# An fp32 transformer kernel on one core: VectorE's product takes the scale of the norm, ScalarE writes only the high part, and the residual is made later

## The reference

```python
for l in range(DEPTH):                      # DEPTH = 2, alpha = 4 ** 0.25
    y = _mla(...) if l == 0 else _swa(...)  # attention, ends with a product o @ w_o
    x = _layernorm(alpha * x + y, ln_mix_g[l], ln_mix_b[l])
    x = _layernorm(alpha * x + _mlp(x, w_up, w_down), ln_mlp_g[l], ln_mlp_b[l])
# _layernorm: (x - mean) * rsqrt(var + eps) * g + b, over the 1024 features
# _mlp: relu(x @ w_up) ** 2 @ w_down
```

## Time and profile before

| | |
|---|---|
| median of three runs | 1906.15 us (1903.37 to 1907.59) |
| the profiled execution, its own time | 1903.75 us |
| its span | 1901.7 us |
| instructions | 22411 |
| VectorE (DVE) busy | 992.5 us, 52% |
| ScalarE (ACT) busy | 663.2 us, 35% |
| GpSimd (POOL) busy | 32.0 us, 2% |
| mean granted clock of TensorE | 0.963 of full speed |

### The profile page before, as it was taken

One profiled execution on the slowest core, in us unless ns is written; L12 is line 12 of the kernel. 1 busy time (PEld: TensorE's weight loads), 2 busy tenths in 40 slices (PEclk: granted clock), 3 DMA queues, 4 the chain that ended last, 5 costly groups with the idle time before them and its releaser, 6 DMA issues.

```text
span 1901.7 us, 22411 instructions
## 1 busy us (share of the span) xinstructions
PE 1818.5 (96%) x9112; PEld 1535.9 (81%) x9112; DVE 992.5 (52%) x1421; ACT 663.2 (35%) x919; POOL 32.0 (2%) x42
## 2 busy tenths in 40 slices
PE   7999989999998999989999999898999999999998
PEld 6787978888888887878888888787878788888886
DVE  3666643434346556653334247655566666256554
ACT  3454341322233446342223133323452322132332
POOL 0000000000000113000000000000000000000000
PEclk9899999999999897999999999897989999999999
DMA  7211223223221110312222322120102222422331
GB/s 270 89 67 45 89 89 111 89 89 110 89 89 67 67 67 1 111 67 102 94 92 88 111 89 89 58 92 28 70 20 84 105 88 93 151 89 91 116 147 67
DMA packets 28287, 169.66 MB, mean 89 GB/s; under 512 B 2800, under 2 KB 7088, under 8 KB 9136
## 3 DMA queue, kind: packets, MB, share of 16 engines
q1 hardware_dynamic: 22448, 156.44, 23.2%
q10 hardware_dynamic: 5760, 12.08, 1.9%
HBM read 166.39 MB, written 5.27 MB: 90 GB/s over the span
## 4 chain that ended last, share of the span: by engine, by line
PE 86%; DVE 7%; ACT 5%; issue 1%; DMA 0%; POOL 0%; DVEq 0%; ACTq 0%
PE ps L1477 28%; PE ps L1479 27%; PE ps L1478 27%; PE ps L1598 2%; DVE w_lo L814 2%; ACT y L562 1%; ACT w_hi L408 1%; ACT s_prob L432 1%; ACT act_hi L570 1%; PE ps L1550 0%; DVE s_pt_lo L814 0%; DVE s_prob L856 0%; PE ps L1872 0%; PE ps L1541 0%; DVE y L965 0%
## 5 line engine op out<-in xcount | busy, mean ns | idle before, releaser
L1477 PE MATMUL ps<-act_hi,w_lo 128*128 128x512 f32 (+1 forms) x1424 | 533.5, 375 | 40.6 <-DVE w_lo L814 22.0
L1478 PE MATMUL ps<-act_hi,w_hi 128*128 128x512 f32 (+1 forms) x1424 | 527.9, 371 | 0.0
L1479 PE MATMUL ps<-act_lo,w_hi 128*128 128x512 f32 (+1 forms) x1424 | 527.8, 371 | 0.0
L408 ACT ACTIVATE w_hi<-stage 128x2048 fp32r<-128x2048 f32 (+4 forms) x147 | 267.3, 1819 | 386.1 <-PE ps L1479 385.4
L814 DVE TENSOR_TENSOR w_lo<-stage,w_hi 128x2048 fp32r<-128x2048 f32 (+5 forms) x151 | 322.5, 2137 | 88.6 <-ACT w_hi L408 88.1
L1477 PEld LDWEIGHTS ps<-act_hi,w_lo 128*128 128x128 f32 x1424 | 272.7, 191 | 89.8 <-issue 28.6
L1479 PEld LDWEIGHTS ps<-act_lo,w_hi 128*128 128x128 f32 x1424 | 272.3, 191 | 45.4
L1478 PEld LDWEIGHTS ps<-act_hi,w_hi 128*128 128x128 f32 x1424 | 272.7, 192 | 44.1
L1477 PE MATMUL ps<-hid_hi,w_lo 128*128 128x512 f32 (+1 forms) x576 | 213.0, 370 | 2.1 <-DVE w_lo L814 2.1
L1479 PE MATMUL ps<-hid_lo,w_hi 128*128 128x512 f32 (+1 forms) x576 | 211.4, 367 | 0.0
L1478 PE MATMUL ps<-hid_hi,w_hi 128*128 128x512 f32 (+1 forms) x576 | 209.7, 364 | 0.0
(11 more groups left out here) (279 smaller groups left out, 2315.5 us busy)
## 6 DMA issues: line engine op xcount, KB each, us to landing
stage<-slabs SPq DMA_DIRECT2D x147, 1024.0 KB, 4.8
bias_rows<-bias_line ACTq DMA_DIRECT2D x1, 3072.0 KB, 19.0
y<-x_t ACTq DMA_DIRECT2D x4, 512.0 KB, 8.4
strips<-bias_rows ACTq DMA_DIRECT2D x2, 1024.0 KB, 6.2
strips<-dilated ACTq DMA_DIRECT2D x2, 1024.0 KB, 5.0
out<-y ACTq DMA_DIRECT2D x4, 512.0 KB, 2.6
stage<-slabs SPq DMA_DIRECT2D x4, 256.0 KB, 7.7
cossin<-rope SPq DMA_DIRECT2D x1, 512.0 KB, 11.6
```

The lines of the kernel that those rows point to most:

```text
L408: nc.scalar.activation(w_hi[p][:, 0:w], stage[s][:, 0:w], ACT.Copy).then_inc(cast_hi, 1)
L1477: mm(out, l_lo, r_hi, start=start, stop=False, skip_group_check=shared)
L1478: mm(out, l_hi, r_hi, start=False, stop=False, skip_group_check=shared)
L1479: return mm(out, l_hi, r_lo, start=False, stop=stop, skip_group_check=shared)
```

## The change

In norms 0, 1 and 2 (all with `last=False`):
- `scale`: for each pair of tiles VectorE runs two `scalar_tensor_tensor` on 128x256, y = y * gain * inverse root, gain being a column of `vec` and the root in PSUM, in place of one 128x512 product.
- `apply`: ScalarE writes `act_hi` = y + offset directly, two 128x256 instructions, in place of two on y, a wait and a 128x512 copy. y no longer gets the offset.
- `lo`: VectorE runs two `scalar_tensor_tensor` on 128x256, `act_lo` = (y + offset) - `act_hi`, in place of one 128x512 subtraction.
- `residual`: behind half 1's `apply`, ScalarE computes a small tile `abeta` = ALPHA * offset (128x8), waits for it, and then runs eight 128x512 instructions y = ALPHA * y + `abeta`. Each waits until VectorE has made the low parts of its pair; the last signals `x_scaled`.
- The out products that were added with the factor ALPHA in the MLPs and before norm 2 are added without it; VectorE waits for `x_scaled` before the first of them. Those before norm 0 keep the factor, as the input x is not scaled.

Norm 3 keeps its instructions.

```diff
+        abeta = keep("abeta", [P, 8])
...
@@ scalar: layer_norm
                     for p in range(4):
                         act.wait_ge(norm_z, 8 * n + 4 * h + p + 1)
+                        if not last:
+                            for t in (2 * p, 2 * p + 1):
+                                ins = nc.scalar.activation(act_hi[:, t, c], y[:, t, c], ACT.Identity,
+                                                           bias=col(beta, t))
+                            ins.then_inc(norm_hi, 1)
+                            continue
                         for t in (2 * p, 2 * p + 1):
                             ins = nc.scalar.activation(y[:, t, c], y[:, t, c], ACT.Identity, bias=col(beta, t),
                                                        scale=col(gain, t))
                         link(ins)
-                        if last:
-                            for t in (2 * p, 2 * p + 1):
-                                ins = nc.scalar.activation(act_hi[:, t, c], y[:, t, c], ACT.Copy,
-                                                           scale=col("g_mix", t))
-                        else:
-                            ins = nc.scalar.activation(act_hi[:, 2 * p:2 * p + 2, c], y[:, 2 * p:2 * p + 2, c],
-                                                       ACT.Copy)
+                        for t in (2 * p, 2 * p + 1):
+                            ins = nc.scalar.activation(act_hi[:, t, c], y[:, t, c], ACT.Copy, scale=col("g_mix", t))
                         ins.then_inc(norm_hi, 1)
+
+                def residual(gen):
+
+                    link(nc.scalar.activation(abeta[:, :], vec[:, VEC[beta]:VEC[beta] + 8], ACT.Copy, scale=ALPHA))
+                    for t in range(KT):
+                        act.wait_ge(act_ready, gen + 8 + 2 * (t // 2) + 2)
+                        ins = nc.scalar.activation(y[:, t, :], y[:, t, :], ACT.Identity, bias=abeta[:, t:t + 1],
+                                                   scale=ALPHA)
+                    ins.then_inc(x_scaled, 1)
...
                 apply(1)
+                if not last:
+                    residual((LN_0, LN_1, LN_2)[n])
@@ vector: layer_norm
                 def scale(h, p):
                     c, bank = half_cols(h), 5 + 2 * h
+                    if not last:
+                        for t in (2 * p, 2 * p + 1):
+                            ins = nc.vector.scalar_tensor_tensor(y[:, t, c], y[:, t, c], col(gain, t),
+                                                                 ps[:, bank, 0:HALF], ALU.mult, ALU.mult)
+                        ins.then_inc(norm_z, 1)
+                        return
...
-                        pair_ = slice(2 * p, 2 * p + 2)
-                        split(act_lo[:, pair_, c], y[:, pair_, c], act_hi[:, pair_, c]).then_inc(act_ready, 2)
+                        for t in (2 * p, 2 * p + 1):
+                            split_scaled(act_lo[:, t, c], y[:, t, c], col(beta, t), act_hi[:, t, c], ALU.add)\
+                                .then_inc(act_ready, 1)
@@ vector: mlp
+                dve.wait_ge(x_scaled, 2 * layer + 1)
                 for j in range(4):
-                    add_out(first + 4 + j, 2 * j, scaled=True)
+                    add_out(first + 4 + j, 2 * j)
@@ vector: the calls
-            layer_norm(SWA_OUT, 2, scaled=True)
+            dve.wait_ge(x_scaled, 2)
+            layer_norm(SWA_OUT, 2, "mix_g1", "mix_b1")
```

More of the change, by code:

```diff
@@ L250, in program @@
         x_landed = [sem(f"x_landed{i}") for i in range(4)]
-        x_hi = sem("x_hi")
+        x_hi, x_scaled = sem("x_hi"), sem("x_scaled")
         const_landed, p_landed = sem("const_landed"), sem("p_landed")
@@ L917, in add_out, with layer_norm @@
                 add(t, slice(0, T), ps[:, b:b + 2, :], scaled).then_inc(slab_read, 1)
-            def layer_norm(first, n, scaled=False, last=False):
+            def layer_norm(first, n, gain, beta, scaled=False, last=False):
                 for j in range(2):
@@ L1156, in _ @@
                 mla_out(u0 + 3)
-            layer_norm(MLA_OUT, 0, scaled=True)
+            layer_norm(MLA_OUT, 0, "mix_g0", "mix_b0", scaled=True)
             mlp(MLP0, 0)
-            layer_norm(MLP0 + 28, 1)
+            layer_norm(MLP0 + 28, 1, "mlp_g0", "mlp_b0")
             g = SWA_KV
@@ L1206, in _ @@
                 swa_out(u0 // 2 + 3)
-            layer_norm(SWA_OUT, 2, scaled=True)
+            dve.wait_ge(x_scaled, 2)
+            layer_norm(SWA_OUT, 2, "mix_g1", "mix_b1")
             mlp(MLP1, 1)
-            layer_norm(MLP1 + 28, 3, last=True)
+            layer_norm(MLP1 + 28, 3, "mlp_g1", "mlp_b1", last=True)
             cast(CONV + 2)
```

## The result

Eleven runs of the changed kernel have a median of 1913.96 us, eleven of the kernel before on the same chip 1903.64 us. The ratio is 1.0045, 95% interval 1.0029 to 1.0061: **slower by 8.6 us** (5.5 to 11.6). The forecast was 1904.8 and a small gain. The profiled execution took 1913.96 us, span 1911.9, against 1903.75 and 1901.7 before.

The account below looks back on a forecast made before the run. TensorE, busy 96% of the span, was taken as the bound, so only its waits around the norms could change: -0.06, -0.85 and -0.36 make -1.3 us, 1904.8 against the median 1906.15. Range 1901.0 to 1910.0.

Parts of the forecast that it names:

- Half 0: First half of norms 0 to 2: the slab's low part starts 7.3 us after the first scale, 0.85 us earlier.
- Norm 1's wait: TensorE's wait for VectorE's add of the last out product: 2.1 instead of 2.98 us, 0.85 gained in full.
- Half 1: Second half of norms 0 to 2: first low part 2.77 us after the scale, TensorE restarting 0.50 us earlier.
- The wait of 0.52: TensorE's wait at 230.10 in norm 0 for a weight slab's low part: 0.52 us gained, likewise in norm 2.
- Slab 49: Behind norm 1: its low part ready 0.46 us later against half 1's scale, TensorE losing and gaining nothing.
- One-column prices: ScalarE instructions with one column operand: 0.91 us a pair for the new high part, 0.63 a residual step.
- The relu: First slab's relu on ScalarE, behind the residual: 0.46 us later in norm 0, 0.16 in norm 2, delaying TensorE's restart.
- the sum of -1.3 us: All terms over the three norms: -0.06 in norm 0, -0.85 in norm 1, -0.36 in norm 2.
- the out products there lose their constant factor: Out products in the MLPs and before norm 2: no TensorE wait ends on one, so costed at nothing.
- ScalarE as the new bound: Rival: residual at two-column price, first relu waits 1.56 us, TensorE's waits 3.8 and 3.5; +5.6, 1911.8 us, chance 0.11.
- The clock falls in the lengthened waits: Rival: waits of 2.9 (norm 0) and 2.6 us (norm 2) lower TensorE's clock; 1906.6 or 1908.3 us, chance 0.25.
- The clock is kept where it fell: Rival: shorter waits, norm 1's 3.52 to 3.0 and norm 2's 4.41 to 3.9, save clock loss; -4.7, 1901.4 us, chance 0.13.

Follow-up runs that it names:

- after_in_place: The changed kernel with abeta in a 64-byte tile replacing table_mark and mark, so later tiles lie as before the change; 1903.35 us, ratio 0.9991 to the kernel before.
- base128: The kernel before with tiles rden and negsink moved to the free end of memory, so hid_hi begins 128 bytes behind a multiple of 2048; 1900.62 us, ratio 0.9986.
- pad32: The kernel before with one unused tile of 128x8 (32 bytes a partition) where the change puts abeta; 1912.06 us, ratio 1.0049.
- late_early: late_residual with the first slab behind each of norms 0 to 2 cast right behind half 1's last parts, ahead of the relu; 1895.74 us, ratio 0.9948 to the kernel before.
- late_residual: after_in_place with ScalarE's eight residual steps moved behind the second up slab's cast (norms 0, 2) or slab 50's (norm 1); 1900.27 us, ratio 0.9978 to the kernel before.
- front32: The kernel before with an unused 32-byte tile ahead of every other tile, moving staging, weight and act tiles too; 1904.41 us, ratio 1.0003.
- act32: The kernel before with act_hi, act_lo, y and the small tiles moved by 32 bytes, weights and hid_hi left in place; 1929.43 us, ratio 1.0129.

## Why the prediction was wrong

**The steps that held.** Half 0: 7.19 us for 7.3. Norm 1's wait: 2.07 us for 2.1, in part by luck. Its release came 0.96 us sooner behind the first scale (601.21 - 589.24 = 11.97, before 12.93) where 0.85 was forecast. In after_in_place that is 11.96, but the wait is 2.38, as TensorE came to it sooner: slab 47 lies in the third pair of weight tiles (see base128), and its triples take 340 ns there and some 355 in the changed kernel, which moved that pair as well. Half 1: the first matmul 2.87 us behind the scale (239.19 to 242.06) for 2.92. The wait of 0.52 gone. Slab 49: TensorE began its product 16.36 us behind the scale of half 1 (626.96 - 610.60), before 16.42 (623.15 - 606.73), so nothing lost and nothing gained, as forecast. One-column prices: 0.91 a pair, residual steps 0.62 apart for 0.63. By the figures of the Trainium skill ("ScalarE: Activation LUTs", under "What ACT_TABLE_LOAD costs") the step is 0.61, an estimate and nearer still; the trace agrees with its rule that each pointer operand adds some 93 ns (a pair 0.91 with one, 1.09 with two). The relu: 0.23 us later in norm 0 for 0.46, since the last high part ended 0.10 sooner than worked out (6.03 behind the scale for 6.13) and the steps took 0.11 less together. With `abeta` in place the sum of -1.3 us met -1.7, interval -3.8 to +0.2.

**The step that failed** is one that the prediction did not price: "the out products there lose their constant factor, with the same elements", "No DMA is added", and nothing on the tile that the change adds. `abeta` is described as a small tile of 128x8, the prediction prices the instruction that writes it, and nowhere is it asked what it moves: the pace of TensorE's products on other tiles was a term put at nothing without a reason. "These waits are all the change can touch" is the sentence that was false: TensorE's pace in products 100 us away could be touched too, through addresses. pad32 shows that this alone costs 9.3 us (6.9 to 11.6), as much as the change lost.

**The rivals.** None of them had this mechanism. The one that ended slower, ScalarE as the new bound, came nearest in time, 1911.8, for a reason that the trace refutes: steps at 0.62 us, the wait at 257.91 at 2.12 us and not 3.8. "The clock falls in the lengthened waits": the wait in norm 0 grew to 2.12 us and not to 2.9, the one in norm 2 not at all, and the clock stayed up behind both. In norm 0 the reason is the clock itself: from 242 to 250 its mean was 0.79 before and is 0.71 now, which makes TensorE some 0.6 us later at the wait. The stretches (us, busy and instructions of PE, PEld, DVE, ACT, POOL, granted clock, DMA share, GB/s) answer to the earlier trace rows:

```profile
242.00:246.00 4.00, 3.94 (x18) 3.97 (x19) 3.81 (x10) 2.57 (x7) 0.00 (x0) 0.50 0.00 0
258.00:262.00 4.00, 4.00 (x18) 3.31 (x19) 2.29 (x3) 2.87 (x2) 0.00 (x0) 1.00 0.71 250
601.00:605.00 4.00, 3.79 (x19) 3.80 (x20) 1.76 (x5) 0.63 (x1) 0.00 (x0) 0.58 0.51 211
613.00:618.00 5.00, 4.53 (x36) 4.44 (x37) 4.36 (x11) 3.37 (x8) 0.00 (x0) 1.00 0.00 0
```

In after_in_place, where norm 2's wait did grow to 2.91 us, the clock did fall behind it, as this rival has it:

```profile
839.00:845.00 6.00, 5.59 (x18) 4.45 (x19) 4.30 (x4) 2.86 (x2) 0.00 (x0) 0.72 0.51 175
```

In the changed kernel the clock fell behind a wait of 2.07 us (601) and stayed behind one of 2.99 (613), where before it had stayed behind 2.98 and fallen behind 3.52. The prediction's reasoning from the longest harmless wait does not hold: the length of one wait does not decide. What does for a single wait, these runs leave open. The Trainium skill's advice against long idle gaps ("TensorE: Matmul & The Clock Gate", under "Why this matters for your kernels") is borne out in part: the falls in these rows came with waits, but the wait of 2.99 us brought none. "The clock is kept where it fell", priced at 1.7 us in norm 1, came true there (613) and gained nothing: TensorE got through the slabs sooner and then waited 1.56 us for slab 49, whose low part comes behind the residual. Over the whole kernel it evened out: mean clock 0.963 before, 0.962 after.

**The range** was wrong for the same cause: it was built from the bounds of terms that held, and had no term for what stood outside them. The 0.12 for slower stood on another cause alone. (The 0.72 for "same" is 0.45, 0.25 and 0.06 less the 0.03 and 0.01 given to the two sides, not 0.01 a side.)

## What to carry to other kernels

A new tile is an edit to every tile allocated after it. Before a change that adds one is judged by its instructions, compare the addresses of the matmul operands, and time the kernel with the tile alone; better, put small tiles into a gap or at the end. When a change costs more than its own stages show, compare the starts of the same event, product by product, over the whole span: a loss that grows by an equal step at products the change does not touch is a change of pace, not a wait.

When engines stand idle behind a stage, look for work whose inputs and place are long free. Here one cast behind each norm, moved ahead of the relu, was worth 5.7 us by the ratios of late_early and late_residual, more than the 1.7 of the arithmetic.

## What the runs showed that was not expected

- TensorE's pace at 128x512 depends on where the streamed operand lies against tiles allocated before it, taken within 2048 bytes: 681 ns for the three matmuls at a distance of 0 from the weights (act; hid in base128: 680), 687 at 320, 700 at 352 and 384, 703 at 416, and some 700 for act at 32. At 128x256 the order differs: 360 ns at 0, 353 at 320 (hid). That 2048 is the period fits all these but was not varied.
- Both operands' places count. front32 moved weights and act together, and nothing changed; act32 moved act and left the weights; and base128 moved the third pair of weight tiles and left act, at 128x256. No run moved the weights alone at 128x512, and why the distance counts is open.
- It is worth as much as the stages that were tuned: 32 bytes ahead of hid cost 9.3 us of 1904, and 32 bytes ahead of act, 24.6.
